# Weight-block sums of the seven-product MLP formed by GpSimd in a program of its own

## What is computed

```python
hn = _rmsnorm(h, g_pre_mlp[l])
u = jnp.square(jax.nn.relu(hn @ w_up[l]))
h = h + _rmsnorm(u @ w_down[l], g_post_mlp[l])
```

## Time and profile before

| | |
|---|---|
| Time, median of 3 runs | 734.73 us (733.27 to 735.40) |
| The profiled execution: its time | 735.45 us |
| The profiled execution: its span | 733.7 us |
| PE busy | 707.8 us, 96% of the span |
| DVE busy | 451.9 us, 62% |
| ACT busy | 366.0 us, 50% |
| POOL busy | 20.8 us, 3% |
| Mean granted TensorE clock | 0.990 |

### The profile page before, as it was taken

How to read it: one execution, slowest core, us unless ns; L and a number is a source line. 1 busy time by engine, 2 the same in 40 slices (tenths; PEclk the granted TensorE clock), 3 DMA queues, 4 the chain that set the end, 5 groups by cost and what they waited for, 6 DMA issues and landing times. The chain is left out here.

```text
span 733.7 us, 10218 instructions
## 1 busy us (share of the span) xinstructions
PE 707.8 (96%) x4182; PEld 568.6 (78%) x4182; DVE 451.9 (62%) x645; ACT 366.0 (50%) x565; POOL 20.8 (3%) x22
## 2 busy tenths in 40 slices
PE   6999999999999989999999999999999799999898
PEld 5889888888655547887887888878887688888687
DVE  3587773356766563256369748694669956429644
ACT  6674553656556554347545444543545333254741
POOL 2000000000002020003000000000000000000000
PEclk9999999999999997999999999999999999999999
DMA  9605333330211002731213251134113033223102
GB/s 351 226 21 192 115 116 116 115 115 1 87 58 45 15 11 105 272 158 53 73 47 116 85 201 58 58 115 173 58 58 115 24 120 115 77 96 114 59 14 101
DMA packets 13838, 74.31 MB, mean 101 GB/s; under 512 B 1824, under 2 KB 3904, under 8 KB 6112
## 3 DMA queue, kind: packets, MB, share of 16 engines
q1 hardware_dynamic: 13392, 70.56, 26.8%
q0 software_dynamic: 256, 3.11, 1.1%
q10 hardware_dynamic: 144, 0.00, 0.0%
HBM read 70.51 MB, written 2.10 MB: 99 GB/s over the span
## 5 line engine op out<-in xcount | busy, mean ns | idle before, releaser
L1639 PE MATMUL bank<-Xhi,Whi 128*128 128x512 f32 (+1 forms) x480 | 187.3, 390 | 2.2 <-DVE Wlo L1452 1.0
L1641 PE MATMUL bank<-Xhi,Wlo 128*128 128x512 f32 (+1 forms) x480 | 185.4, 386 | 0.0
L1640 PE MATMUL bank<-Xlo,Whi 128*128 128x512 f32 (+1 forms) x480 | 185.3, 386 | 0.0
L1639 PE MATMUL bank<-Whi,Uhi 128*128 128x512 f32 (+1 forms) x304 | 118.3, 389 | 4.1 <-DVE Wlo L1116 3.9
L1640 PE MATMUL bank<-Wlo,Uhi 128*128 128x512 f32 (+1 forms) x304 | 115.7, 381 | 0.0
L1641 PE MATMUL bank<-Whi,Ulo 128*128 128x512 f32 (+1 forms) x304 | 115.6, 380 | 0.0
L1639 PEld LDWEIGHTS bank<-Xhi,Whi 128*128 128x128 f32 x480 | 90.2, 188 | 26.3 <-issue 6.9
L1641 PEld LDWEIGHTS bank<-Xhi,Wlo 128*128 128x128 f32 x480 | 90.2, 188 | 18.3
L1640 PEld LDWEIGHTS bank<-Xlo,Whi 128*128 128x128 f32 x480 | 90.2, 188 | 17.1
L1107 DVE TENSOR_TENSOR Wlo<-raw,Whi 128x2048 fp32r<-128x2048 f32 x28 | 64.1, 2290 | 51.5 <-ACT Whi L729 51.5
L729 ACT ACTIVATE Whi<-raw 128x2048 fp32r<-128x2048 f32 x30 | 57.4, 1913 | 43.9 <-PE bank L1641 35.2
(11 more groups left out here) (232 smaller groups left out, 885.4 us busy)
## 6 DMA issues: line engine op xcount, KB each, us to landing
raw<-wst SPq DMA_DIRECT2D x43, 1024.0 KB, 4.8
arena<-wst SPq DMA_DIRECT2D x16, 1024.0 KB, 4.9
arena<-ctab POOLq DMA_DIRECT2D x1, 2880.0 KB, 9.9
arena<-xn SPq DMA_DIRECT2D x4, 512.0 KB, 5.7
arena<-xn SPq DMA_DIRECT2D x1, 2048.0 KB, 7.8
out<-arena SPq DMA_DIRECT2D x7, 256.0 KB, 2.0
arena<-gpost SPq DMA_DIRECT2D x2, 512.0 KB, 6.3
arena<-arena SPq DMA_DIRECT2D x8, 64.0 KB, 2.0
```

The lines of the kernel that those rows point to most:

```text
L1639: mm(out_ap, w[0], x[0], start=start, stop=False, **kw)
L1640: mm(out_ap, w[0], x[1], start=False, stop=False, **kw)
L1641: return mm(out_ap, w[1], x[0], start=False, stop=stop, **kw)
```

## The change

`weight_sum` moves from DVE's program to the end of GpSimd's, with the same waits, now made by GpSimd, and the same output slots. GpSimd does the fifteen sums one after another in the order of their numbers; DVE's list loses them at the places where they stood.

```diff
@@ gpsimd
             nc.gpsimd.memset(EX, 0.0).then_inc(acc_zero, 1)
+            def weight_sum(q, into, one, other, op, loads, count):
+                for name in loads:
+                    pool.wait_ge(*IN[q, name])
+                if count > 1:
+                    pool.wait_ge(wsum, 5 * q + count - 1)
+                elif q:
+                    pool.wait_ge(use_lo, USE[q - 1, 7] + 1)
+                else:
+                    pool.wait_ge(lo_done, G_OUT + 4)
+                if count in (3, 4):
+                    pool.wait_ge(use_lo, USE[q, 3 if count == 3 else 2] + 1)
+                nc.gpsimd.tensor_tensor(at_slot(q, into), at_slot(q, one), at_slot(q, other), op).then_inc(wsum, 1)
+
+            for q in range(PAIRED):
+                weight_sum(q, "P", "R", "Q", ALU.subtract, ("b12", "b22"), 1)
+                weight_sum(q, "R", "S", "R", ALU.add, ("b11",), 2)
+                weight_sum(q, "P", "S", "Q", ALU.add, (), 3)
+                weight_sum(q, "S", "T", "S", ALU.subtract, ("b21",), 4)
+                weight_sum(q, "T", "T", "Q", ALU.add, (), 5)
@@ vector
-                V2.tensor_tensor(at_slot(q, into), at_slot(q, one), at_slot(q, other), op).then_inc(wsum, 1)
...
                     left_low(p, 7, 0)
-                    weight_sum(p, "S", "T", "S", ALU.subtract, ("b21",), 4)
                     use_low(q, "u1")
-                    weight_sum(p, "T", "T", "Q", ALU.add, (), 5)
                     accumulate(p, 5)
...
                 left_low(q, 6, 0)
-                weight_sum(q, "P", "R", "Q", ALU.subtract, ("b12", "b22"), 1)
                 if q:
                     use_low(q, "u3")
-                weight_sum(q, "R", "S", "R", ALU.add, ("b11",), 2)
...
                 left_low(q, 6, 1)
-                weight_sum(q, "P", "S", "Q", ALU.add, (), 3)
                 use_low(q, 6)
...
             q = PAIRED - 1
-            weight_sum(q, "S", "T", "S", ALU.subtract, ("b21",), 4)
             accumulate(q, 1)
...
             left_low(q, 7, 0)
-            weight_sum(q, "T", "T", "Q", ALU.add, (), 5)
             accumulate(q, 5)
```

## The result

The changed kernel takes 774.53 us (median of 4 runs, 769.46 to 774.83) against 735.05 us (4 runs, 733.27 to 735.40): a ratio of 1.0524, 95% interval 1.0496 to 1.0552. It is slower by 39 us; forecast were 772.3 us and a range of 755 to 783.

A forecast was written before the change was run, and what follows sets the result against it. VectorE's panel splits were taken to make TensorE wait only 3.9 us, all else hidden behind matmuls; -3.9 + 27.3 + 9.0 + 5.2 = +37.6 us gave 772.3 us against the median, range 755 to 783.

The forecast's parts named there:

- Sums 4 and 5, three pairs: At product 1 of each pair, two GpSimd sums hold VectorE 4.56 us each, delaying split and TensorE 9.1 us: +27.3 us.
- Sums 1 and 2, two pairs: At u3 of the second and third pair, GpSimd's sums delay the split TensorE needs by 4.5 us each: +9.0 us.
- The two waits at the end: In the last pair, TensorE's two waits for a VectorE panel split vanish once the sums leave VectorE: -3.9 us.
- The granted clock, with small rests: TensorE's clock drops behind five new waits, 1.3 us each, less 1.3 us for the spell that goes: +5.2 us.
- The reading of the two small holds: Two small VectorE SBUF-only instructions ended with GpSimd's subtractions, so GpSimd's sums should hold such VectorE instructions until finished.
- Who goes first: With GpSimd waiting and VectorE's next instruction ready, GpSimd was assumed to go first, having asked earlier; chance 0.50.
- the rival in which VectorE goes first: GpSimd gets in only at VectorE's accumulations or idle time: 3.4 us per late split, 756 to 763 us; chance 0.30.
- The slack of each place: Time between a split's end and its matmuls: none at product 1, 0.9 us at u3 of the second pair.
- sum 3: Third weight sum of each pair, forecast to cost nothing because VectorE's 5.04 us idle before product 6's split covers one hold.
- The other row: Low clock at 275.6 to 284.5 us, 4.4 us lost; used for the three long waits, the clock term becomes +14.5.
- The faster rival: SBUF port free often enough that VectorE loses nothing; the waits and the 1.2 GHz spell vanish: 729.5 us, chance 0.06.

## Why the prediction was right

By its own steps, against the profiled execution, whose span grew by 38.5 us:

| Term | forecast | measured | read from |
|---|---|---|---|
| Sums 4 and 5, three pairs | +27.3 | +26.2 | three waits of 8.74 or 8.75 us |
| Sums 1 and 2, two pairs | +9.0 | +8.1 | two waits of 4.03 us |
| The two waits at the end | -3.9 | -3.9 | gone from PE's waits |
| The granted clock, with small rests | +5.2 | +8.1 | 38.5 less the three above |
| Sum | +37.6 | +38.5 | |

That the sum came within 1 us is luck in part: the waits were forecast 2.0 us too high and the clock 2.9 us too low.

*The reading of the two small holds* carried the case. From a TENSOR_SCALAR of 1.97 us and a one-element TENSOR_TENSOR of 4.00 us it followed that splits, left sums and left pieces would be held and accumulations not. The changed kernel shows it with 5.64, 5.00 and 0.68 us. The runs with writes alone and with a copy show that it hangs on GpSimd reading SBUF. The Trainium skill, SBUF — State Buffer, section "Who interferes with whom", says that a VectorE instruction with two SBUF inputs contends with a GpSimd instruction that reads SBUF, "not with one that only writes it"; the trace agrees, 690 ns for a left piece in the mean of the run with 5.6 us of writes per sum. The TENSOR_SCALAR of the earlier trace rows, recorded with one tensor input, was held too; no run tests that kind of instruction.

*Who goes first* was the one price that no row before showed, and it is now shown: left piece, GpSimd, left sum, GpSimd, left piece. GpSimd got in behind the instruction in flight each time, and VectorE got exactly one between two sums. Whether GpSimd has precedence, or was first because it asked before VectorE's next instruction was issued, the runs don't tell apart. The waits of 8.7 and 4.0 us rule out the rival in which VectorE goes first. Each hold was 4.3 to 4.4 us and not the 4.56 of the forecast, which is why three waits came to 26.2 and not 27.3 us.

*The slack of each place* was right: none at product 1, little at u3, and TensorE has no wait at any other place where a sum runs. The 4.5 us at u3 were 4.03, and sum 3 was free.

*The clock* was the term that was mis-sized: 1.3 us for each wait was taken from the short spell behind the second wait at the end, and 1.5 to 2.3 us came out, 9.4 in all; less the 1.3 of the spell that is gone that is the 8.1. The other row gave 4.4 us for the long waits, which would have been much too high: the long ones cost 1.5 to 2.0 us and the short ones 2.2 and 2.3. The total of 8.1 lies inside the ends of 5.2 and 14.5. The clock also varies between executions of one kernel: that of 769.46 us had a mean clock of 0.973, the others 0.965. Why was not tried.

*The faster rival* (729.5 us if VectorE lost nothing) had the right price, as the run without sums shows with 729.3, but its condition did not hold.

## What to carry to other kernels

GpSimd is not a free helper for VectorE: while it read SBUF here, VectorE's instructions with two SBUF inputs stood still until it was done (4.4 us beside a sum, 1.7 beside a copy), and it went ahead of those that were next. Give it such work only in idle time of VectorE, by an explicit wait that releases it there, or choose work that only writes. First ask what a sum costs where it is: here thirteen of fifteen were already hidden, and the last two were better handled by an early slot, a second load and an adding DMA than by another engine. And when two variants differ by a few microseconds, compare the stretch that was changed, not only the total: the total carries spells of low clock from elsewhere.

## What was not expected of the hardware

- Size does not protect an instruction: a VectorE TENSOR_TENSOR on four elements per partition, 0.16 us before, was held for the whole first sum (POOL from 348.35 to 352.97).

```profile
348.34 4.64 DVE L1491 TENSOR_TENSOR st<-st 128x4 f32<-128x4 f32 x1
```

- A GpSimd instruction's recorded time seems to include its wait for VectorE: 4.6 us where VectorE was idle or just starting, 4.9 to 5.4 us where it was in the middle of such an instruction, and 1.9 against 2.2 to 2.8 us for the copy.
- A DMA that adds onto SBUF took 11.5 us for 1 MB, 2.4 times a plain load of 4.8 us. It is a single transfer, issued by POOL where the plain loads are issued by SP; what each of the two differences costs was not tried. It held no instruction of VectorE: from 558 to 570 us splits took 2.28 us, the left sum 1.22, left pieces 0.68 or 0.69.
- A shorter wait of TensorE did not cost less clock: behind waits of 8.7 us 1.5 to 2.0 us were lost, behind waits of 4.0 us 2.2 and 2.3.
